# RWKV scan: direction 1 on the off-diagonal 64x64 tiles, alternating with direction 0, and the turn of X behind the next lower product

## What is computed

```python
def rwkv7_scan(r, w, k, v, kk, a, state):
    def step(s, inp):
        r_t, w_t, k_t, v_t, kk_t, a_t = inp
        sa = jnp.einsum('bhvk,bhk->bhv', s, kk_t)
        s = s * w_t[:, :, None, :] - sa[..., None] * (kk_t * a_t)[:, :, None, :] + v_t[..., None] * k_t[:, :, None, :]
        return s, jnp.einsum('bhvk,bhk->bhv', s, r_t)
...
    for d in range(2):
        bwd = d == 1
        yc, s_ctx = rwkv7_scan(*[maybe_flip(t, 1, bwd) for t in (rc, wc[:, :, d], kc[:, :, d], vc, kkc, ac[:, :, d])], zero)
        yl, _ = rwkv7_scan(*[maybe_flip(t, 1, bwd) for t in (rl, wl[:, :, d], kl[:, :, d], vl, kkl, al[:, :, d])], s_ctx)
```

## Time and profile before

| | us |
|---|---|
| median of 3 runs (lowest, highest) | 4583.22 (4576.23, 4587.27) |
| span of the profiled execution | 4582.6 |
| TensorE matmul busy, whole span | 4244.7 (93%) |
| VectorE, ScalarE, GpSimd busy | 1832.9, 1337.3, 370.5 |
| mean granted TensorE clock | 0.961 |
| RWKV scan, layer 0 (first matmul to last) | 1344.2 to about 1710 |
| RWKV scan, layer 1 | 3719.9 to 4089.9 |

### The profile page before, as it was taken

The page is one execution under the profiler, slowest core; times in us unless marked ns, Lnnn a source line. Parts: engine busy times, 40 slices in busy tenths (PEclk is TensorE's granted clock), DMA queues, the critical chain, the costliest instruction groups (busy, mean ns, idle before and its releaser), DMA issues. The chain is left out here.

```text
span 4582.6 us, 108171 instructions
## 1 busy us (share of the span) xinstructions
PE 4244.7 (93%) x47197; PEld 3798.5 (83%) x47197; DVE 1832.9 (40%) x2815; ACT 1337.3 (29%) x1972; POOL 370.5 (8%) x637
## 2 busy tenths in 40 slices
PE   6999989899869998999998999989999869988998
PEld 5999977898749996989897999977898659976886
DVE  3222236454474444322224222255454464444334
ACT  3211124333352222411123211133332432233222
POOL 1000000231001100010101000000330001100000
PEclk8999999999979999999999999999999879999999
DMA  6232331000200002242423222121002000013332
GB/s 204 81 112 89 101 122 51 24 2 19 59 1 4 4 20 96 68 164 65 165 65 120 64 64 64 57 67 47 16 2 63 14 2 4 4 62 83 92 101 65
DMA packets 344271, 287.40 MB, mean 63 GB/s; under 512 B 9086, under 2 KB 316772, under 8 KB 343396
## 3 DMA queue, kind: packets, MB, share of 16 engines
q1 hardware_dynamic: 326628, 218.92, 16.0%
q0 software_dynamic: 17280, 62.92, 3.9%
HBM read 270.27 MB, written 11.53 MB: 61 GB/s over the span
## 5 line engine op out<-in xcount | busy, mean ns | idle before, releaser
L655 PE MATMUL PS<-x_hi,w_hi 128*128 128x384 f32 (+1 forms) x2464 | 677.3, 344 | 17.2 <-DVE x_lo L559 16.1
L655 PE MATMUL PS<-x_hi,w_lo 128*128 128x384 f32 (+1 forms) x2464 | 676.0, 343 | 0.0
L655 PE MATMUL PS<-x_lo,w_hi 128*128 128x384 f32 (+1 forms) x2464 | 675.9, 343 | 0.0
L655 PEld LDWEIGHTS PS<-x_hi,w_hi 128*128 128x128 f32 x2464 | 450.4, 189 | 38.6 <-issue 24.4
L655 PEld LDWEIGHTS PS<-x_lo,w_hi 128*128 128x128 f32 x2464 | 450.1, 189 | 13.8
L655 PEld LDWEIGHTS PS<-x_hi,w_lo 128*128 128x128 f32 x2464 | 449.8, 189 | 13.9
L788 DVE TENSOR_TENSOR silu_buf<-silu_buf,PS 128x768 f32<-128x768 f32 (+1 forms) x88 | 78.1, 888 | 785.9 <-ACT silu_buf L721 785.9
L699 PE MATMUL PS<-hidden_hi,w_hi 128*128 128x256 f32 (+1 forms) x1232 | 347.9, 353 | 19.4 <-DVE hidden_lo L793 19.4
L631 DVE TENSOR_TENSOR w_lo<-raw_w,w_hi 128x2048 fp32r<-128x2048 f32 x136 | 311.7, 2292 | 133.7 <-ACT w_hi L626 133.7
L626 ACT ACTIVATE w_hi<-raw_w 128x2048 fp32r<-128x2048 f32 x136 | 259.6, 1909 | 340.2 <-PE PS L699 333.1
L699 PE MATMUL PS<-hidden_hi,w_lo 128*128 128x256 f32 (+1 forms) x1232 | 340.4, 346 | 0.0
(11 more groups left out here) (331 smaller groups left out, 7287.5 us busy)
## 6 DMA issues: line engine op xcount, KB each, us to landing
raw_w<-in_ffn_w_dram SPq DMA_DIRECT2D x240, 512.0 KB, 4.4
arena<-in_ada_w_dram POOLq DMA_DIRECT2D x120, 512.0 KB, 6.1
arena<-in_w_in_dram SPq DMA_DIRECT2D x64, 512.0 KB, 3.9
arena<-in_ada_w_dram SPq DMA_DIRECT2D x6, 2048.0 KB, 14.2
raw_w<-in_ffn_w_dram SPq DMA_DIRECT2D x32, 384.0 KB, 3.4
arena<-in_w_out_dram SPq DMA_DIRECT2D x16, 512.0 KB, 4.1
h_save<-arena SPq DMA_DIRECT2D x16, 384.0 KB, 2.3
arena<-h_save SPq DMA_DIRECT2D x2, 3072.0 KB, 15.6
```

Of the source, the lines that this page charges most:

```text
L655: mm = pe.matmul(PS[:, 4 * b + 2 * g + s, 0:half], w[wo][:, k, g, :], x_split[xo][:, k, a + s * half:a + (s + 1) * half], start=(k == 0 an ...
```

## The change

1. **Tiles.** Direction 1 goes to the off-diagonal tiles: its products read partitions 0 to 63 and write PSUM partitions 64 to 127, or the reverse (`lands`). Each group now runs over `LANES`, that is both directions and both halves, for each u: four matmuls in a row on four tiles. In groups that sum two or three products into one place (`state_on_keys`, `state`, `output`), the first products of all four come first, then the second ones.
2. **Banks and semaphores.** The two directions of a result lie in neighbouring banks (2b and 2b + 1), and one instruction of VectorE or ScalarE takes both, of twice the size; one semaphore stands for both. The state of direction 1 lies in the other half of the partitions than its keys, so that SyncE copies `KKR` of direction 1 across by two DMAs a chunk (`sp_rw`, `kkr_across`), and the decays once a layer on VectorE (`pc_across`).
3. **Order.** `lower_times_x` of level l + 1 stands ahead of `turn_x` of level l. The turned X of level 0 is made by TensorE and ScalarE (`turn_x(0)`, `move_y(0)`) instead of VectorE.
4. **Masks.** A packed copy of the level masks is made by 24 GpSimd copies in the setup; `pair_spread`, which nothing used, goes. GpSimd's copies of a chunk stand in the order in which they are wanted, behind one wait for both directions. `level_counts` brings the semaphores that are no longer used to the values that the next layer's DeltaNet stage expects.

```diff
+        OTHER = {0: HALVES[1], 64: HALVES[0]}
+        def sp_rw(sp, layer):
+            for c in range(RW_CHUNKS):
+                it = rw_counts(layer, c)[0]
+                sp.wait_ge(kk_copied[1], it + 1)
+                sp.wait_ge(r_copied[1], it + 1)
+                sp.wait_ge(rw_o_summed, it)
+                for p in HALVES:
+                    sp.dma_start(kkr_across[OTHER[p.start]], KKR[c % 2][1][p]).then_inc(kkr_crossed, 16)
...
+        LANES = [(g, p) for g in range(2) for p in HALVES]
+        def lands(g, p):
+            return p if g == 0 else OTHER[p.start]
...
                 for u in range(NB):
-                    for p in HALVES:
-                        mm = pe.matmul(PS[p, bank_, at + u * width:at + (u + 1) * width], lhs(u)[p], rhs(u)[p],
+                    for g, p in LANES:
+                        mm = pe.matmul(PS[lands(g, p), 2 * bank_ + g, at + u * width:at + (u + 1) * width], lhs(g, u)[p], rhs(g, u)[p],
                                        start=True, stop=True)
...
                 def state():
-                    for g in range(2):
-                        pe.wait_ge(vn_ready[g], it + 1)
+                    pe.wait_ge(rw_vn_ready, it + 1)
+                    for g in range(2):
                         pe.wait_ge(kb_moved[g], it + 1)
-                        for u in range(NB):
-                            for p in HALVES:
-                                o = PS[p, 4 * g + 3, u * D:(u + 1) * D]
-                                pe.matmul(o, kbt[g][p, 0, u, :], vtk[g][p, u, :], start=True, stop=False)
-                                mm = pe.matmul(o, kbt[g][p, 1, u, :], U_T[g][p, u, :], start=False, stop=True)
-                        mm.then_inc(s_summed[g], 1)
+                    for u in range(NB):
+                        for g, p in LANES:
+                            pe.matmul(PS[p, 6 + g, u * D:(u + 1) * D], kbt[g][p, 0, u, :], vtk[g][p, u, :], start=True, stop=False)
+                        for g, p in LANES:
+                            mm = pe.matmul(PS[p, 6 + g, u * D:(u + 1) * D], kbt[g][p, 1, u, :], U_T[g][p, u, :],
+                                           start=False, stop=True)
+                    mm.then_inc(rw_s_summed, 1)
...
                 def move_y(l):
-                    for g in range(2):
-                        act.wait_ge(x_turned[g], xt2 + l)
-                        act.wait_ge(xd_summed[g], ts2 + l)
-                        sc.activation(YR[r][g], half_bank(4 * g + 1), ACT.Copy).then_inc(y_ready[g], 1)
+                    act.wait_ge(rw_x_turned, xs2 + l + 1)
+                    if l > 0:
+                        act.wait_ge(rw_xd_summed, ts2 + l)
+                    sc.activation(wide(YR2[r]), both_banks(1), ACT.Copy).then_inc(rw_y_ready, 1)
...
+                def first_x():
+                    dve.wait_ge(rw_a_summed, it2 + 1)
+                    dve.wait_ge(rw_x_turned, xs2)
+                    v.tensor_tensor(XR2, both_banks(2).rearrange("p g (u t) -> p g u t", u=NB), over(lower0), ALU.mult).then_inc(rw_x0_step, 1)
+                    dve.wait_ge(rw_x0_step, it2 + 1)
+                    v.tensor_tensor(XR2, XR2, over(id_c[:, :]), ALU.add).then_inc(rw_x_ready, 1)
+                def mask_b():
+                    dve.wait_ge(rw_br_summed, it2 + 1)
+                    v.tensor_tensor(ABR2[r], keyed(2), over(ab_mask), ALU.mult).then_inc(rw_br_masked, 1)
```

More of the change, by code:

```diff
@@ L1941, in build, with rw_both @@
         ab_mask, ak_mask = region(26880, 2 * D), region(27008, 2 * D)
-        lower0, lower0_t = (region(27136 + 64 * n, D) for n in range(2))
-        level_c = level[:, 1:LEVELS_RW, :]
+        kkr_across, lower0, pc_across = region(27136, NB, 2 * D), region(48896, D), region(48960, NB, RW_CHUNKS)
+        def rw_both(start, *dims):
+            n = dims[0] * dims[1] * (dims[2] if len(dims) > 2 else 1)
+            return [region(start + 2 * q * n, 2, *dims) for q in range(2)]
+        ST2, VTK2, YR2, ABR2 = rw_both(17408, NB, D), rw_both(21504, NB, D), rw_both(32768, NB, D), rw_both(30720, NB, 2 * D)
@@ L1957, in rw_counts @@
             ts = TS * layer + 6 * (LEVELS_DN - 1) + (LEVELS_RW - 1) * c
-            xt = ts
-            return it, own, xs, ts, xt
+            return it, own, xs, ts, xs + Y_MORE * (layer + 1)
         def rw_walk(eng, step):
@@ new lines, in state_on_keys @@
+                    pe.wait_ge(kkr_crossed, CROSSED0 + 32 * (own + 1))
+                    for u in range(NB):
+                        for g, p in LANES:
+                            pe.matmul(PS[lands(g, p), 6 + g, u * D:(u + 1) * D], kkr[g][p, u, 0:D], S[g][p, u, :],
+                                      start=True, stop=False)
+                        for g, p in LANES:
+                            mm = pe.matmul(PS[lands(g, p), 6 + g, u * D:(u + 1) * D], akr[g][p, u, 0:D], vtk[g][p, u, :],
+                                           start=False, stop=True)
@@ new lines, in output @@
+                def output():
+                    pe.wait_ge(rw_s_added, it + 1)
+                    for u in range(NB):
+                        for g, p in LANES:
+                            pe.matmul(PS[lands(g, p), 6 + g, u * D:(u + 1) * D], S[g][p, u, :], kkr[g][p, u, D:2 * D],
+                                      start=True, stop=False)
+                        for g, p in LANES:
+                            pe.matmul(PS[lands(g, p), 6 + g, u * D:(u + 1) * D], vtk[g][p, u, :], akr[g][p, u, D:2 * D],
+                                      start=False, stop=False)
+                        for g, p in LANES:
+                            mm = pe.matmul(PS[lands(g, p), 6 + g, u * D:(u + 1) * D], U_T[g][p, u, :], abr[g][p, u, D:2 * D],
+                                           start=False, stop=True)
+                    mm.then_inc(rw_o_summed, 1)
@@ L2098, in x_times_lower @@
[L2098 to L2109 removed]
+                    pe.wait_ge(rw_x_ready, xs2 + l)
@@ new lines, in lower_times_x @@
+                    if l == 1:
+                        pe.wait_ge(rw_br_masked, it2 + 1)
+                    for u in range(NB):
+                        for g, p in LANES:
+                            o = PS[lands(g, p), g, 0:128].rearrange("p (u b j) -> p u b j", u=NB, j=1 << l)[:, u]
+                            mm = pe.matmul(o, abr2[g][p, u, 0:D], even(XR[g][p, u, :], l, "p"), start=True, stop=True)
+                    mm.then_inc(rw_tx_summed, 1)
+                def x_times_lower(l):
+                    pe.wait_ge(rw_tx_masked, ts2 + l)
+                    pe.wait_ge(rw_y_ready, ys2 + l)
+                    times(1, 0, D // 2, lambda g, u: y2[g][:, u, :], lambda g, u: TR[g][:, u, :]).then_inc(rw_xd_summed, 1)
@@ L2219, in dve_rw, with over, keyed @@
             dve.wait_ge(masks_made, 2 * layer + 2)
+            def over(mask):
+                return mask.unsqueeze(1).unsqueeze(1).broadcast_to([P, 2, NB, mask.shape[1]])
+            def keyed(b):
+                return PS[:, 2 * b:2 * b + 2, :].rearrange("p g (u t) -> p g u t", u=NB)
             def step(c, q, at, more):
                 if c is not None:
-                    it, own, xs, ts, xt = rw_counts(layer, c)
+                    it, own, xs, ts, ys = rw_counts(layer, c)
                 if more:
@@ L2550, in _ @@
                 sp_proj_rw(sp, layer)
+                dma_after(sp, start_of(layer, 6))
+                sp_rw(sp, layer)
                 dma_after(sp, start_of(layer, 7))
```

303 lines of the change are left out of this document (136 added, 167 removed).

## The result

The changed kernel takes 4597.24 us (median of 6 runs, 4588.3 to 4602.99), the kernel before 4585.61 in the same comparison: ratio 1.0028, 95% interval 1.0017 to 1.0038. It is slower by 0.3%, where I had forecast 4393 us. The profiled execution of the changed kernel took 4588.3 us, with a span of 4586.3 and a mean granted clock of 0.935. One step of the forecast was wrong, and nearly all of the 190 us went with it: **TensorE's instructions don't come fast enough for four tiles.**

A forecast was written before the change was run, and what follows sets the result against it. TensorE's matmuls bound the scan; 14.9 us of work plus 6.9 us of open waits make a 21.8 us chunk against 30.25, saving 95 us a layer, 190 in both: 4583 - 190 = 4393 us, eight in ten 4355 to 4475.

The forecast's parts named there:

- What bounds it now: RWKV scan: TensorE's matmuls bound it, near 29 ns a narrow record on two tiles, 30.25 us a chunk.
- The rate, first question: Whether matmuls on four tiles overlap in the scan: yes, taken as 14.6 ns a narrow record, 28 a wide one.
- The rate, second question: Whether TensorE's instructions come fast enough: yes, 25 ns or less a product, where four tiles need one in 29 ns.
- half-way rival: Supply or bank conflicts in the scan give about 20 ns a record, 27 us a chunk: about 4510 us, chance 0.10.
- TensorE's work in a chunk: Scan: 896 narrow records at 14.6 ns and 64 wide at 28 ns, 14.9 us a chunk.
- Open waits: TensorE's uncovered waits for VectorE and ScalarE in the scan, with both directions merged: 6.9 us a chunk.
- the rival of turns: Four tiles only take turns, two running at once: 35.3 us a chunk, 4698 us, chance 0.09.
- The crossing and the setup: SyncE's two DMAs a chunk land before the state product wants them, and GpSimd's added setup copies cost 0.
- The clock rival: TensorE's clock falls to 1.2 GHz for one stretch a chunk, about 1.5 us each: 4430 us, chance 0.10.
- The floor rival: Starts over all tiles cannot follow closer than 25 ns: 30.4 us a chunk, 4587 us, chance 0.03.
- the forecast's weighing: Both diagonal tiles write one PSUM bank; 29 ns against 58 ns speak against the skill's rule that they run in turns.
- The signs: Changed scan: chunks 21.8 us apart; groups of 32 records in 0.47 us; TensorE idle before X products 6-7 us; clock 1.00.

The follow-up runs named there:

- burst (b): Kernel before with 512 products of 32 columns on two tiles, written out without waits, behind the scan of layer 0: 29.2 ns a record.
- burst (a): Kernel before with 512 products of 32 columns on four tiles, written out without waits, behind the scan of layer 0: 27.9 us for 1024 records.
- e3: Changed kernel with each scan product over two heads' columns, so half the matmuls and weight loads, and other values: 4352.74 us in a single run.
- e1: Changed kernel with direction 1 back on the diagonal tiles, so two tiles, all else of the change kept: 4730.21 us, ratio 1.0323.
- e2: Changed kernel with ten added products of 384 columns a chunk, never read, put where TensorE waits: 4595.11 us, ratio 1.0031.
- the bursts: Kernel before with stretches of products without any wait, written out or in loops, added behind the scan of layer 0; written out, 3.5 us a packet.
- e11: Changed kernel with each turn by TensorE issued twice, 288 records a chunk more: 4782.39 us (2 runs).
- burst (d): Kernel before with 32-column products on four tiles in a loop of 64 turns of 16, behind the scan of layer 0: 19.4 ns a record.

## Why the prediction was wrong, step by step

- **What bounds it now:** the pace of two tiles was right as far as it went: 29.1 ns, and 29.2 in burst (b). What I did not see is how near the next bound lay. The trace of before had it: 81 packets in 11 chunks, 7.4 a chunk. At the predicted 21.8 us a chunk each of 7.5 packets would have had 2.9 us. I never put that beside the queue of instructions.
- **The rate, first question:** right. Three tiles side by side in the earlier trace rows did mean four, 14.6 ns.
- **The rate, second question: this is the step that failed.** I took "whether the instructions come fast enough" from two waits of TensorE's sequencer 0.2 us apart with 8 products of the program between them, which is 12.5 ns a record. That reading is true of instructions already in stock (burst (a) ran its first 186 at 14.7 ns), and I used it for the supply that fills the stock, 27.3 ns a record once the stock is used up. The rate term was 14.6 ns where 27.3 held: 960 x 0.0273 = 26.2 us a chunk instead of 14.9. The chunk took 31; the runs don't part what the open waits and what the lower clock behind the stops add to the 26.2. The half-way rival did name the supply, but with 20 ns a record.
- **TensorE's work in a chunk:** one slip, small. Not all of direction 1 goes to the off-diagonal tiles: `state` stays on the diagonal ones for both directions (its results land on `p`, not on `lands(g, p)`), and I priced it at 14.6 ns. In the changed kernel 8 of its records take 0.23 us:

```profile
1598.07 0.40 PE L2083 MATMUL PS<-arena 64*64 64x64 f32 x8
1598.30 0.40 PE L2085 MATMUL PS<-arena 64*64 64x64 f32 x8
```

  64 records at 29 ns are 0.93 us a chunk more. The wide records' 28 ns held: 8 in 0.22 us in e3.
- **Open waits:** 6.9 us forecast, 5.4 of TensorE's idle time in e3, which counts from the end of the last record, 0.2 us behind its start, some eight times a chunk. Chunk 20.4 against 21.8, once the supply is out of the way; with the lesser work of e3 (12.2 us) the same sum would have been 19.1, so it is right to 7% from either side, and no closer test of it was run. And merging with two tiles costs 6 us (e1), as the rival of turns had it (35.3 forecast, 36.2 measured).
- **The crossing and the setup:** right. No wait of TensorE names a DMA at the state product; the copies landed in 2.4 us by the DMA view.
- **The clock rival:** a fallen clock came (0.83 in the scan), but not from the cause that I gave: with the open waits alone it stayed at 0.98 (e3). What it costs isn't shown, since the products that brought it back in e2 took some 3 us a chunk of their own. I had priced it as though it were added to the rest, where it falls together with the supply.
- **The floor rival (4587 us, chance 0.03):** it named the right size, 25 ns for every start, and nearly the right time. The reason it gave was another one, a floor on starts, which the 14.6 ns disprove. By the Trainium skill, "TensorE: Matmul & The Clock Gate", section "Wait — 56ns, not 53.3ns?", a start would take about 25 ns at least; the 96 records in 1.40 us don't agree with that for starts on different tiles.
- **The Trainium skill, "TensorEngine Tiling (Array Packing)", Gotcha 1** (different row tiles cannot access one PSUM bank at the same time): by it the pairs would have taken turns. Rows 0 to 63 and 64 to 127 write different partitions of one bank here, and the trace after shows them 14.6 ns apart, so the forecast's weighing stands.
- **The signs:** "groups of 32 in 0.47" and "idle before the X products" came true, "21.8 us apart" and "clock at 1.00" didn't. The list had no sign for a stop in the middle of a group, because no rival stopped there.

What stays open: why the scan of the changed kernel takes 4.1 us a packet and the bursts 3.5. In some stretches TensorE asks for less, at the lower level of the clock and in open waits, and no run separates the two. With twice the turns (e11) it is 3.9. How much of the 31 us would come back if the clock stayed up at no cost is open as well, down to the 26.2 us that the supply sets. Why a packet starts 3.5 us behind the last, when it is on its way for 1.1, no run shows. None of the runs that compute all of the reference beats the kernel before.

## What to carry to other kernels

Before you make a written-out stretch of TensorE denser, count its instructions (matmuls and weight loads, and twice as many for fp32) and divide the time that you hope for by their number of packets, 256 instructions each. In these runs no longer written-out stretch got under 3.5 us for a packet, 27 ns for a matmul with its load, and in the changed kernel with its waits it was 4.1. Many small matmuls hit that before they hit the array. The waits in the trace of before don't warn, though it sits only 7% above it; its count of fetched packets does. Fewer and wider instructions took the stops away (e3), and a loop with a body of up to 64 KB did without fetches in the bursts, at some 0.15 us a turn; no loop was tried in the scan. More tiles alone, a clock brought back by added products or one group of turns less did not beat the kernel before.

## What was not expected of the hardware

- Instructions of TensorE are fetched in packets of 16 KB, 256 instructions; a written-out burst got one per 3.5 us, though each is on its way for only 1.1, and "issue" gaps of up to 1.9 us inside a group are its mark. A loop body of 64 KB was fetched once, one of 128 KB in every turn.
- A switch between transposes and products, both fp32 on 64x64 tiles, costs 0.15 to 0.18 us each way at a granted clock of 1.00; with every second product of the turns a transpose, the kernel before was 18.75% slower, its clock in the scan down to 0.68 as well.
- In burst (a) the clock stayed at 1.2 GHz while narrow records followed each other on four tiles without a gap, after the first two "issue" gaps:

```profile
1763.20:1777.00 13.80, 13.80 (x512) 0.50 0.02 5
```

  yet in burst (d), without a gap at its start, the same records ran at 2.4 GHz for 39.8 us. In the changed kernel, two stretches at the lower level, with "issue" gaps ahead of each:

```profile
1430.30:1440.50 10.20, 8.12 (x240) 0.50 0.02 5
1450.80:1474.70 23.90, 19.43 (x640) 0.50 0.02 4
```
